# Six PSUM banks in rotation, moved turns and waits, and running sums as two products, in a two-block transformer kernel

## The reference

```
# first block
h  = rmsnorm(x) * (1 + scale) + shift                  # scale, shift, gate from silu(c) @ mod_w
cq, ckv, kr, gq, gk, gv, gate = split(h @ ab_w_in)     # stage in1, 2336 columns
qa = rmsnorm(cq) @ w_uq;  kv = rmsnorm(ckv) @ w_ukv    # the "latents" cq, ckv; stage up
... rmsnorm per head, rotary, attention mla and gqa, x + gate * (mix @ ab_w_out)
... second layer: windowed attention win, a short convolution, x + gate * (mix @ cd_w_out)
# second block
qa, ka, va, qb, kb, vb, f_logit, z = split(rms_norm(h) @ w_in_even)
oa = diff_attention(qa, ka, va)                        # attention "diff"
cum_logf = cumsum(log_sigmoid(f_logit + b_forget), axis=tokens)
ob = fox_attention(qb, kb, vb, cum_logf)               # scores + cum_logf[q] - cum_logf[k]
h = h + (concat(oa, ob) * silu(z)) @ w_out_even
h = h + (p @ w_ple) * sigmoid(h @ w_gate)              # after each layer
q, k, v, z = split(rms_norm(h) @ w_in_odd)
q = rope(rms_norm(q, qn)) ; k = rope(rms_norm(k, kn))  # per head, 8 heads of 128
o = dilated windows of q, k, v                         # attention "odd"
h = h + (o * silu(z)) @ w_out_odd
```

## Time and profile before

| | us |
|---|---|
| median of 3 runs | 1699.04 |
| lowest and highest run | 1697.67, 1699.29 |
| the profiled execution, its own time | 1707.18 |
| span of the profile | 1705.4 |
| TensorE busy | 1609.5 |
| VectorE busy | 898.1 |
| ScalarE busy | 649.6 |
| GpSimd busy | 565.6 |
| granted TensorE clock, mean | 0.969 |

### The profile page before, as it was taken

One profiled execution on the slowest core, in us unless ns is written; L12 is line 12 of the kernel. 1 busy time (PEld: TensorE's weight loads), 2 busy tenths in 40 slices (PEclk: granted clock), 3 DMA queues, 4 the chain that ended last, 5 costly groups with the idle time before them and its releaser, 6 DMA issues.

```text
span 1705.4 us, 25046 instructions
## 1 busy us (share of the span) xinstructions
PE 1609.5 (94%) x9248; PEld 1348.2 (79%) x9248; DVE 898.1 (53%) x2089; ACT 649.6 (38%) x1328; POOL 565.6 (33%) x333
## 2 busy tenths in 40 slices
PE   4999899899999979999999999999999999899998
PEld 1788888698998858878888789966688778687787
DVE  2565737656665244932643778047521389806422
ACT  3322354245554223324642433444423333226332
POOL 1132231860001323446615344400534534431134
PEclk8999999789999989999999999979999999999999
DMA  8322123122103112321003232300023222310222
GB/s 324 89 62 58 53 61 88 54 84 62 39 26 125 50 43 69 99 87 50 26 14 98 78 99 84 91 1 26 26 74 93 91 80 94 99 62 1 86 88 86
DMA packets 93158, 124.41 MB, mean 73 GB/s; under 512 B 10288, under 2 KB 52208, under 8 KB 92016
## 3 DMA queue, kind: packets, MB, share of 16 engines
q1 hardware_dynamic: 93040, 122.82, 22.8%
HBM read 120.70 MB, written 2.10 MB: 72 GB/s over the span
## 4 chain that ended last, share of the span: by engine, by line
PE 79%; DVE 14%; ACT 3%; issue 2%; DMA 1%; POOL 0%; SPq 0%; DVEq 0%; ACTq 0%; POOLq 0%
PE psum L869 16%; PE psum L871 16%; PE psum L870 16%; PE psum L1082 9%; PE psum L1070 5%; PE psum L993 3%; PE psum L1047 3%; PE psum L839 3%; DVE squares L1433 2%; DMA mod_w<-mod_w_in 1%; PE psum L1040 1%; PE psum L1043 1%; PE psum L930 1%; DVE ssq L1435 1%; PE psum L1041 1%
## 5 line engine op out<-in xcount | busy, mean ns | idle before, releaser
L1820 POOL TENSOR_TENSOR wlo<-wraw,whi 128x1024 fp32r<-128x1024 f32 (+4 forms) x172 | 399.1, 2322 | 968.2 <-ACT whi L1133 968.1
L1133 ACT ACTIVATE whi<-wraw 128x1024 fp32r<-128x1024 f32 (+4 forms) x172 | 175.1, 1019 | 494.7 <-PE psum L871 491.8
L869 PE MATMUL psum<-whi,h2h 128*128 128x512 f32 (+2 forms) x800 | 311.9, 390 | 6.9 <-ACT buf L1182 5.8
L870 PE MATMUL psum<-wlo,h2h 128*128 128x512 f32 (+2 forms) x800 | 307.3, 384 | 0.0
L871 PE MATMUL psum<-whi,h2l 128*128 128x512 f32 (+2 forms) x800 | 307.3, 384 | 0.0
L869 PE MATMUL psum<-whi,hTh 128*128 128x512 f32 (+2 forms) x512 | 197.0, 385 | 8.9 <-DVE hTl L1523 7.3
L871 PE MATMUL psum<-whi,hTl 128*128 128x512 f32 (+2 forms) x512 | 192.3, 376 | 0.0
L870 PE MATMUL psum<-wlo,hTh 128*128 128x512 f32 (+2 forms) x512 | 192.1, 375 | 0.0
L1279 ACT ACTIVATE pr<-psum,nmax 128x768 f32<-128x768 f32 (+2 forms) x208 | 138.1, 664 | 128.8 <-DVE nmax L1619 85.0
L869 PEld LDWEIGHTS psum<-whi,h2h 128*128 128x128 f32 x800 | 152.0, 190 | 33.0 <-issue 7.9
L871 PEld LDWEIGHTS psum<-whi,h2l 128*128 128x128 f32 x800 | 151.8, 190 | 27.4
(11 more groups left out here) (264 smaller groups left out, 2618.4 us busy)
## 6 DMA issues: line engine op xcount, KB each, us to landing
wraw<-mod_w_in SPq DMA_DIRECT2D x32, 512.0 KB, 3.8
wraw<-w_in_odd_in SPq DMA_DIRECT2D x32, 512.0 KB, 3.5
wraw<-cd_w_in_in SPq DMA_DIRECT2D x24, 512.0 KB, 3.6
wraw<-w_in_even_in SPq DMA_DIRECT2D x20, 512.0 KB, 3.9
mod_w<-mod_w_in SPq DMA_DIRECT2D x8, 1024.0 KB, 17.8
wraw<-ab_w_in_in SPq DMA_DIRECT2D x16, 512.0 KB, 3.6
wraw<-w_ple_gate_in SPq DMA_DIRECT2D x16, 512.0 KB, 3.8
wraw<-ab_w_out_in SPq DMA_DIRECT2D x8, 512.0 KB, 3.8
```

Of the source, the lines that this page charges most:

```text
L869: eng.matmul(dst, a[0], ww[0], start=first, stop=False)
L870: eng.matmul(dst, a[0], ww[1], start=False, stop=False)
L1133: eng.activation(whi[:, s, :, 0:w], wraw[:, u["id"] % RAW, :, 0:w], ACT.Copy).then_inc(*to("split_hi", u["id"]))
L1820: eng.tensor_tensor(wlo[:, s, :, 0:w], wraw[:, u["id"] % RAW, :, 0:w], f32(whi[:, s, :, 0:w]), ALU.subtract)\
```

## The change

Four edits. (1) Each chunk gets a list of banks of its own: over a run of stages that follow each other without an attention, the next chunk takes the next free ones of banks 0 to 5 in rotation, so that chunks of six tiles keep banks 0 to 5 and chunks of four start at 0, 4, 2, 0 and so on. The last chunk ahead of an attention gets 2, 3 in place of 0, 1 for its last two tiles. (2) VectorE's low parts of the latents' turns move from behind the gq norm to between its tiles 2 and 3. (3) The first head of odd waits for the norms of k0 and q0 alone, and the preps of head 4 wait for those of k1 and q1. (4) The running sums are two products of 16 columns, the triangular matrix and the matrix of ones by all of `fneg`; VectorE adds the tiles' totals in three operations.

```diff
         def stage(name, items):
             ST[name] = [plan.chunk(...) for i, it in enumerate(items)]
-            for i, c in enumerate(ST[name]):
-                c["bank"] = 0 if c["split"] else i % 6
...
+        following = {"up": "gqa", "in2": "win", "in3": "diff", "in4": "odd"}
+        runs = (("in1", "up"), ("out1", "in2"), ("out2", "in3"), ("out3", "sig3", "ple3", "in4"), ("out4", "sig4", "ple4"))
+        for run in runs:
+            first_bank = 0
+            for name in run:
+                for c in ST[name]:
+                    c["banks"] = [(first_bank + n_) % 6 for n_ in range(len(c["tiles"]))]
+                    first_bank += len(c["tiles"])
+                    if c is ST[name][-1] and name in following and c["banks"][2:] == [0, 1]:
+                        c["banks"][2:] = [2, 3]
...
-                        b = c["bank"] + n_
+                        b = c["banks"][n_]
...
             def running_sums():
...
                 bank_free(7)
-                for t in XT:
-                    for b in range(t + 1):
-                        mm = eng.matmul(psum[:, 7, t * 4:t * 4 + 4], tri if b == t else ones, fneg[:, b, :],
-                                        start=b == 0, stop=b == t)
+                gates = fneg[:, :, :].rearrange("p t h -> p (t h)")
+                eng.matmul(psum[:, 7, 0:16], tri, gates, start=True, stop=True)
+                mm = eng.matmul(psum[:, 7, 16:32], ones, gates, start=True, stop=True)
...
-                "odd": [("vector", ("normed", n_, t)) for n_ in ("q0", "q1", "k0", "k1") for t in XT]}
+                "odd": [("vector", ("normed", n_, t)) for n_ in ("k0", "q0") for t in XT]}
...
+                if name == "odd" and key[1] == 4:
+                    for t in XT:
+                        eng.wait_ge(*at("vector", ("normed", key[0] + "1", t)))
...
                 eng.wait_ge(*at("cumsum", 0))
                 after_last()
-                cum = psum[:, 7, 0:16].rearrange("p (t h) -> p t h", t=NX)
-                eng.tensor_scalar(fcum[:, :, :, 0], cum, -1.0, None, ALU.mult).then_inc(*small())
-                eng.tensor_copy(fcum[:, :, :, 3], cum).then_inc(*note("vector", ("fcum",)))
+                within, whole = (psum[:, 7, a:a + 16].rearrange("p (t h) -> p t h", t=NX) for a in (0, 16))
+                eng.tensor_copy(fcum[:, :, :, 3], within).then_inc(*small())
+                for b in range(NX - 1):
+                    after_last()
+                    eng.tensor_tensor(fcum[:, b + 1:NX, :, 3], fcum[:, b + 1:NX, :, 3],
+                                      whole[:, b:b + 1, :].broadcast_to([P, NX - 1 - b, 4]), ALU.add).then_inc(*note("vector", ("sums", b)))
+                after_last()
+                eng.tensor_scalar(fcum[:, :, :, 0], fcum[:, :, :, 3], -1.0, None, ALU.mult).then_inc(*note("vector", ("fcum",)))
...
-            for n_ in ("cq", "ckv", "gk", "gq"):
+            for n_ in ("cq", "ckv", "gk"):
                 norm(n_)
-            products("in1", 4)
-            products("up", 0)
+            norm_stats("gq", ALL)
+            for i, t in enumerate(ALL):
+                if i == 3:
+                    products("in1", 4)
+                    products("up", 0)
+                norm_scale("gq", t, i)
+                norm_rope("gq", t)
```

More of the change, by code:

```diff
@@ L268, in mod_stage @@
             for c, (i, m) in zip(ST[name], parts):
-                c["layer"], c["tile"], c["bank"] = i, m, 7
+                c["layer"], c["tile"], c["banks"] = i, m, [7]
         def mod_w(k):
@@ L922, in modulation_unit @@
             def modulation_unit(c):
-                b, u = c["bank"], c["units"][0]
+                b, u = c["banks"][0], c["units"][0]
                 eng.wait_ge(*at(f"load_w{u['id'] % RAW}", u["id"]))
@@ L934, in turn_modulation @@
             def turn_modulation(c):
-                b = c["bank"]
+                b = c["banks"][0]
                 eng.wait_ge(*at("mod_rows", c["name"]))
@@ L1163, in evacuate @@
             def evacuate(c, t, n_):
-                b, w, kind = c["bank"] + n_, c["width"], c["evac"][1]
+                b, w, kind = c["banks"][n_], c["width"], c["evac"][1]
                 eng.wait_ge(*at("product", (c["name"], t)))
@@ L1310, in mod_rows @@
                 eng.wait_ge(*at("unit_used", c["units"][-1]["id"]))
-                eng.activation(mod_row[:, :], psum[:, c["bank"], 0:P], ACT.Copy).then_inc(*to("mod_rows", c["name"]))
+                eng.activation(mod_row[:, :], psum[:, c["banks"][0], 0:P], ACT.Copy).then_inc(*to("mod_rows", c["name"]))
             def spread(i, s_, j):
```

## The result

| | before | changed |
|---|---|---|
| median of 8 runs each, us | 1702.28 | 1682.14 |
| lowest and highest run | 1697.67, 1713.90 | 1678.09, 1690.23 |
| profiled execution, its own time | 1707.18 | 1682.29 |
| span of the profile | 1705.4 | 1680.5 |

The ratio is 0.9874, with a 95% interval of 0.9837 to 0.9911: the changed kernel is faster, by 20.1 us between the medians and by 24.9 us between the two profiled spans. The forecast was a gain of 31.3 us and 1667.7 us. The time lies 14.4 us above it, 3.2 of them because the median of before rose from 1699.04 to 1702.28 with more runs.

The account below looks back on a forecast made before the run. TensorE, busy 94% of the span and 79% of the chain, was taken as the bound, through idling, work and clock. Terms 5.6 + 6.4 + 9.2 + 10.1 = 31.3 us off the 1699.0 median gave 1667.7 us, range 1659 to 1686.

Parts of the forecast that it names:

- 1. The latents' turns: At the latents' turns in bank 6, TensorE's wait and the low clock behind it go: 5.6 us, ends 2.5 and 7.8.
- The price: VectorE norms gq tiles 3 to 5 only after the turns, until 215.1: a new 0.8 us stall ahead of up2.
- the half fall: Behind the new stall ahead of up2, one fall of the clock costs 2.8 us; half of it was counted.
- 2. Banks: Second chunks of in3, in4 and in2 stop waiting for evacuations: 3.3, 1.9 and 1.2 us, sum 6.4, ends 1 and 9.
- 3. Waits of the last attention: Ahead of in46, the 6.40 us wait for k1's norm and 2.8 us of low clock go: 9.2 us, ends 6 and 10.
- The cover: Last attention: first-head copies are needed about 1525, 35 us later than k1, so VectorE's later norms hold nothing up.
- 4. Running sums: In diff, fewer products and no low clock gain 10.1 us; 2.1 us if the clock falls; 10.1 likelier, 6 to 4.
- rival A: The clock still falls in diff, or unprofiled runs before lacked that fall: gain 23.3 us, time 1675.7; chance 0.27.
- B: Split or VectorE takes over: a large stall returns one step later, worst in in4, 9.2 us, time 1676.9; chance 0.12.
- C: Changing banks lowers TensorE's clock in four-tile chunks, 3.0 us each; eleven eat the gain, fifteen give 1713 us; chance 0.05.
- D: Stalls go but each clock fall moves to the new wait near it: gain 13.2 us, time 1685.8; chance 0.10.

Follow-up runs that it names:

- the kernel with four products: The changed kernel with the running sums as four products that add up in PSUM and VectorE's two operations of before: 1681.75 us, ratio 0.9862.
- part 3 alone: The kernel before with only the last attention's waits for its norms split by halves: 1694.03 us, ratio 0.9941 to before.
- part 2 alone: The kernel before with only the rotation of banks: 1705.99 us, ratio 1.0005 to before.
- parts 1, 3 or 4 alone: The kernel before with only the latents' turns moved, only the last attention's waits split, or only the sums as two products: 1695.47, 1694.03, 1703.21 us.
- the one made to test it: The changed kernel with gq tile 3 between the latents' turns, four accumulating products, and rotation in in3 and in4 alone: 1676.32 us, ratio 0.9840.

## Why the prediction was right, and where it was wrong

The direction held, and so did the range (1659 to 1686), which was wide enough for most of the rivals; the likeliest case (1667.7) did not come. By its own steps:

**1. The latents' turns**, forecast 5.6 us, measured 3.0 from the first of these turns to gqa in both profiles (3.7 and 4.7 with what lies ahead of them). Up starts 8.4 and 9.3 us earlier instead of 7.8, but 0.7 and 1.6 us of that were there before the turns began. The price, norms done at 215.1, was right to 0.1 us, by two deviations that cancel. The stall was 1.6 us instead of 0.8, and the half fall that I took was a whole one, 3.0 us, in both profiles; in the kernel with four products, where it did not come, the same stretch takes 41.6 us, 5.9 less than before. The end named for VectorE's norms "stretched by another 1.7 us by the splits" came true in part: the one stretched operation grew from 1.95 to 2.51 us.

**2. Banks**, forecast 3.3 + 1.9 + 1.2. In3 gave 3.3 and 3.2 us, in2 1.2 and 1.1. In4 gave 8.1 with part 3, where part 3 alone gave 6.5: 1.6. The trade of each wait for one of the low part was right, and so was that in4's share is hidden behind k1 without part 3 (0.1 us in part 2 alone). What I put at nothing was the effect on win and out2, which have the same instructions: 3.6 + 1.1 us given back in one profile, 1.5 + 0.1 in the other. The new waits kept the clock up, as I took them to, and that is most of what in3 gained: with parts 1, 3 or 4 alone, which leave its old wait and 3.4 us of low clock, it takes 183.7 us against 181.8. That nothing is gained by this part alone (1.0005) is the case for which I cited the Trainium skill, TensorE: Matmul & The Clock Gate, section HAM oscillation. The traces show another reason than none to gain: 4.6 us are gained and paid back by the clock.

**3. Waits of the last attention**, forecast 9.2 us, measured 9.1 alone and, with 1.6 of part 2, 10.7 in the change. The cover held: k1's norms and the copies were not waited for.

**4. Running sums**, forecast 10.1 us with the clock up, measured 3.6. This step failed, by 6.5 us, the largest miss; and against kernels with the ten products and the clock low for equally long, part 4 gives 0.9 us. Its parts were nearly right: 0.8 us for the bank, 0.6 for the products (0.7 forecast), 1.9 for fcum (1.6). What failed is "I take 10.1 as likelier": I read the low clock as the work of the 3.40 us of four-column products, and it came all the same with 0.6 us of them, about the end of the wait for fcum. With four products and a wait of 1.0 to 1.2 us it came too. In 13 profiles of kernels other than before, it never stayed away there; only its length changed, from 3.4 to 20.5 us. The whole is rival A, "the clock still falls in diff". Its price, 2.1 us of gain, took the low stretch to be as long as before: too low for the changed kernel (3.6, low for 13.7 us) and for those low for 3.4 us (8.5), and too high at equal length (0.9). What sets the length is open.

**Sum.** 1.9 (part 1) + 6.5 (part 4) + 0.4 (parts 2 and 3) = 8.8 us make 22.5 out of the forecast 31.3. The stages with unchanged instructions gained another 2.2 us by the clock, which makes the span's 24.9 but for rounding. The medians gained less, 20.1, because the profile of before is 4.9 us slower than its median and that of the changed kernel lies at its own.

**The rivals.** B came in its small form, waits for the split in in31 and in41, and not in its large: none of 9.2 us came back. C, rotation slows the products, did not come as put: the chunks of in3 and in4 run at 1.00 with the rotation in the nine profiles that have it. The Trainium skill, TensorE: Matmul & The Clock Gate, section A second HAM failure mode, tells of another kernel whose clock went down and up as it cycled through banks; in these chunks the traces show nothing of it. The loss from the rotation lies in an attention 43 us behind the last rotated chunk. D, each fall moves to the wait near it, came for parts 1 and 4 (falls at the new stall ahead of up2 and at the wait for fcum) and not for parts 2 and 3, whose falls went; what it didn't have is that falls come and go in stages that nobody touched.

## What to carry to other kernels

Read a stage whose instructions did not change before you credit or blame an edit: here such stages moved by up to 11 us. Sum the waits and the work at full clock, and take the clock as a term of its own with its own spread (here 1501 us per 1.0 of mean clock, some 10 us of the gain). At the stalls that the change takes away the low clock went with the stall where that was long (2.8 to 8.0 us here): it was there in every profile with the stall and in none without. At one of 1 to 2 us amid turns it depends also on what came before, and an edit upstream can bring it or take it. Where two engines' work meets at one buffer, freeing the buffer or changing the order only passes the wait on to the other supplier: what is gained is the difference of their lateness.

## What the runs showed of the hardware

- Behind the same wait of 1.6 us in the same code the clock was at 1.2 GHz for 6.8 us in six profiles and not in a seventh; it ended 168.5 to 169.2 us after the last rise in the six profiles with a fall and 170.0 us in the one without. In win, 196.6 to 197.9 against 198.9 to 199.3 us, over 13 profiles, and 199.0 without a fall in the one made to test it. Why these distances and not others is open; so is why the runs of one kernel can differ by 16 us (1678.8 to 1695.2 us).
- Gqa took 151.8 to 163.5 us with the same instructions, low for 6.8 to 30.7 us.
- A VectorE operation with two SBUF inputs of 256 columns took 2.51 us instead of 0.41 beside a GpSimd operation of 2.44 us. Its neighbours ahead of GpSimd's start took 0.42 and 0.43. I had costed this only as an end of the range.
